# Seven half-size products for most pairs of the first layer's up tiles, and another order of attention's instructions, in a two-layer transformer kernel on one core

## The chip, the core and the metric

The kernel runs on one core of one Trainium2 chip. A core has five engines that each work through their own list of instructions in order: TensorE (PE, with its weight loads as PEld), VectorE (DVE), ScalarE (ACT), GpSimd (POOL) and SyncE (SP), which here only issues DMAs. They wait for each other by semaphores. The metric is the device time of one execution, in microseconds (us).

## The reference, cut to what matters

Two layers run over 768 tokens of 1024 features: 512 latent tokens and 256 context tokens. The second layer gives up the context tokens after its attention projections. The part that changes most is the channel sub-layer of the first layer:

```python
u = h @ w_up                                   # 768 x 1024 times 1024 x 5632
u = depthwise_conv3(u) + conv_b                # along the tokens
g, v = jnp.split(u, 2, axis=-1)                # 22 tiles of 128 gates, 22 of values
x = x + gate * ((jax.nn.silu(g) * v) @ w_down) # 2816 -> 1024
```

The mixing sub-layer before it (projections, grouped-query attention with 8 heads, differential attention with 4 heads, output projection) runs in both layers. Everything is float32. A layer's modulation (`adaLN`) is a product of a 1024-vector with 1024 x 6144 weights, of which most tiles are computed on VectorE beside other work.

## The kernel before

**Layout.** Features lie on the 128 partitions and tokens along the free dimension, so a tile of an activation is 128 x 768: tokens 0 to 511 (one PSUM bank) and 512 to 767 (another). There are eight banks of 512 floats, so four such pairs of banks.

**Float32 by three products.** TensorE takes each operand rounded (`fp32r`), so every operand is split in two: a high half made by ScalarE (`w_hi`, `h_hi`, `a_hi`: a copy that rounds) and a low half made by a subtraction (`w_lo` on GpSimd, line 1136; `h_lo` and `a_lo` on VectorE, lines 2255 and 2622). One product is then three matmuls, high by high, low by high and high by low: helper `three`, lines 1254 to 1256.

**The weight stream.** Units of 128 x 1024 floats (512 KB) come from HBM by SP (`load_unit`, line 1020) into two raw buffers `w_raw`. ScalarE makes `w_hi` (line 1700) and GpSimd `w_lo` in a ring of four. SP loads the next unit into a raw buffer when `w_lo` of the one in it is made. A unit is the weights of one 128-feature up tile, or of one down tile.

**The channel sub-layer.** `PARTS = [8, 8, 6]`: three times in a layer, `n` pairs of a gate tile and a value tile go up, and then eight down tiles sum over those `n` pairs. An up tile is `feature_unit`: for each of the two token groups, 8 k-tiles of three matmuls. For each pair (`pairs`, ScalarE from line 2061 and VectorE from line 2595):

- ScalarE: `conv_g` and `conv_v` from PSUM with the middle tap and the bias (line 2070), after `a_lo` of the pair before; then the next units' `w_hi`; the SiLU (line 2077) and `a_hi` (line 2079).
- VectorE: the outer taps, four instructions for a tile (line 2610); the product of gate and value (line 2619); `a_lo` (line 2622); and one tile of the modulation weights against two vectors (`ada_tile`, line 2117), whose 512 KB SP loads (line 1024) in its one queue with the weights.
- After the part's pairs, VectorE adds each down tile to `x_sb` (`update`, line 2560), with more tiles of the modulation beside it.

In the last part the last four down tiles (`tail_units`) are made for the first token group first, so that the norm of that group can begin while TensorE does the second.

**Attention.** `mixing_plan` writes down each operation of the mixing sub-layer with its engine, a duration, a preferred position and what it needs, and places them one by one: always the operation that can begin first, by those durations and a delay of .06 or .09 us for a signal. The order so found is what the four engines' lists contain. All waits are semaphores on what an operation needs, so the durations in the plan decide the order and nothing else.

## Time and profile before

| | us |
|---|---|
| median of 3 runs (1761.12 to 1761.82) | 1761.22 |
| the profiled execution | 1760.48 |
| its span in the profile | 1758.7 |
| PE busy | 1658.7 (94%) |
| DVE busy | 1120.0 (64%) |
| ACT busy | 769.9 (44%) |
| POOL busy | 617.5 (35%) |
| channel sub-layer of layer 0, stretch 480 to 1034 | 554 |
| attention of layer 0, stretch 105 to 405 | 300 |
| attention of layer 1, stretch 1063 to 1340 | 277 |

Busy is the time in which an engine had an instruction in work. Matmuls overlap each other in the profile, and their ends are modelled, so the pace of TensorE is read from the distance between the starts of two matmuls, not from the duration of one.

### The profile page before, as it was taken

How to read it: one execution, taken by the hardware profiler on the slowest of the kernel's cores; microseconds unless marked ns; L12 is line 12 of the kernel's file. 1: busy time of each engine (PE TensorE's matmuls, PEld its weight loads, DVE VectorE, ACT ScalarE, POOL GpSimd, SP SyncE). 2: the span in 40 equal slices, each digit the busy share in tenths (PEclk: the TensorE clock that was granted, in tenths of full speed). 3: DMA queues.
4: the chain of work that ended last, by engine and by line, in shares of the span. 5: the costliest groups of instructions: out<-in, count | busy, mean ns of one | idle time of the engine just before them, and what ended most of it. 6: DMA issues, size and time to landing. Idle time of an engine off the chain costs nothing.

```text
span 1758.7 us, 25943 instructions
## 1 busy us (share of the span) xinstructions
PE 1658.7 (94%) x9530; PEld 1403.9 (80%) x9530; DVE 1120.0 (64%) x1749; ACT 769.9 (44%) x1273; POOL 617.5 (35%) x311
## 2 busy tenths in 40 slices
PE   5999998889799999999999998999888999999997
PEld 3778786778688888888888886888666888888887
DVE  7986677677876575767245774677664864254256
ACT  6546676463253311332123344666554543243242
POOL 0356560210123243323422307564222154444442
PEclk9899999999899999999999999999999999999999
DMA  9520000024222333433434423000012133233232
GB/s 393 178 93 25 25 25 13 25 109 150 90 96 87 116 121 108 134 117 120 144 120 131 144 96 96 25 25 25 25 37 96 48 120 97 94 95 106 87 99 91
DMA packets 45533, 168.24 MB, mean 96 GB/s; under 512 B 4736, under 2 KB 6784, under 8 KB 43520
## 3 DMA queue, kind: packets, MB, share of 16 engines
q1 hardware_dynamic: 40896, 156.50, 26.4%
q10 hardware_dynamic: 4544, 10.49, 1.6%
q8 instruction: 60, 0.98, 0.2%
q14 instruction: 33, 0.27, 0.0%
HBM read 161.73 MB, written 5.24 MB: 95 GB/s over the span
## 4 chain that ended last, share of the span: by engine, by line
PE 73%; DVE 7%; issue 3%; ACT 2%; POOL 1%; DMA 1%; DVEq 0%; ACTq 0%; SPq 0%; POOLq 0%
PE ps L1254 22%; PE ps L1255 21%; PE ps L1256 21%; PE ps L1385 3%; PE ps L1399 2%; DVE junk_mid L2150 1%; PE ps L1418 1%; DVE sqsum L2220 1%; DVE nb L2408 1%; PE ps L1419 1%; DVE p_sb L2426 1%; POOL w_lo L1136 1%; ACT ptmp L1919 1%; DMA w_raw<-w_d 1%; DVE ht L2247 0%
## 5 line engine op out<-in xcount | busy, mean ns | idle before, releaser
L1136 POOL TENSOR_TENSOR w_lo<-w_raw,w_hi 128x1024 fp32r<-128x1024 f32 x175 | 444.3, 2541 | 933.2 <-ACT w_hi L1700 893.9
L1254 PE MATMUL ps<-h_hi,w_hi 128*128 128x512 f32 (+1 forms) x1592 | 570.3, 358 | 14.5 <-DVE h_lo L2255 6.8
L1255 PE MATMUL ps<-h_lo,w_hi 128*128 128x512 f32 (+1 forms) x1592 | 558.8, 351 | 0.0
L1256 PE MATMUL ps<-h_hi,w_lo 128*128 128x512 f32 (+1 forms) x1592 | 558.4, 351 | 0.0
L1254 PEld LDWEIGHTS ps<-h_hi,w_hi 128*128 128x128 f32 x1592 | 304.6, 191 | 63.4 <-issue 24.7
L1256 PEld LDWEIGHTS ps<-h_hi,w_lo 128*128 128x128 f32 x1592 | 304.2, 191 | 39.9
L1255 PEld LDWEIGHTS ps<-h_lo,w_hi 128*128 128x128 f32 x1592 | 305.1, 192 | 35.5
L1700 ACT ACTIVATE w_hi<-w_raw 128x1024 fp32r<-128x1024 f32 x188 | 198.3, 1056 | 240.8 <-PE ps L1256 222.5
L1254 PE MATMUL ps<-a_hi,w_hi 128*128 128x512 f32 (+1 forms) x552 | 191.8, 347 | 1.2 <-DVE a_lo L2622 1.2
L1255 PE MATMUL ps<-a_lo,w_hi 128*128 128x512 f32 (+1 forms) x552 | 191.5, 347 | 0.0
L1256 PE MATMUL ps<-a_hi,w_lo 128*128 128x512 f32 (+1 forms) x552 | 191.1, 346 | 0.0
L2610 DVE SCALAR_TENSOR_TENSOR conv_v<-ps,sm,conv_v 128x511 f32<-128x511 f32 (+1 forms) x132 | 83.2, 658 | 141.4 <-ACT conv_v L2070 135.1
L2408 DVE TENSOR_REDUCE nb<-ps 128x1 f32<-128x768 f32 (+1 forms) x160 | 129.1, 845 | 29.4 <-PE ps L1385 28.9
L1176 POOL TENSOR_TENSOR p_sb<-p_sb,ri 128x768 f32<-128x768 f32 (+1 forms) x80 | 107.5, 1363 | 93.5 <-DVE ri L2415 93.5
L2433 DVE TENSOR_TENSOR pt_lo<-ps,pt_hi 128x512 fp32r<-128x512 f32 (+1 forms) x160 | 106.3, 675 | 43.2 <-ACT pt_hi L1929 41.9
L2610 DVE SCALAR_TENSOR_TENSOR conv_g<-ps,sm,conv_g 128x511 f32<-128x511 f32 (+1 forms) x132 | 83.1, 658 | 68.9 <-ACT conv_g L2070 57.5
L1929 ACT ACTIVATE pt_hi<-ps 128x512 fp32r<-128x512 f32 (+1 forms) x160 | 91.9, 586 | 76.0 <-PE ps L1399 75.2
L2560 DVE SCALAR_TENSOR_TENSOR x_sb<-ps,mod,x_sb 128x512 f32<-128x512 f32 x72 | 45.3, 657 | 123.5 <-PE ps L1256 123.2
L2117 DVE CUSTOM_DVE_ANT_0 ada_junk<-ada_b,c_bc 128x1024 bf16<-128x1024 f32 x80 | 117.0, 1463 | 2.0 <-DMA ada_b<-ada_d 0.7
L1919 ACT ACTIVATE p_sb<-ps,nb 128x768 f32<-128x768 f32 (+1 forms) x120 | 97.0, 813 | 46.8 <-DVE nb L2408 43.3
L2070 ACT ACTIVATE conv_v<-ps,sm 128x512 f32<-128x512 f32 x66 | 44.2, 705 | 167.0 <-PE ps L1256 167.0
L1254 PEld LDWEIGHTS ps<-a_hi,w_hi 128*128 128x128 f32 x552 | 104.6, 190 | 14.7 <-DVE a_lo L2622 1.6
(186 smaller groups left out, 2414.1 us busy)
## 6 DMA issues: line engine op xcount, KB each, us to landing
w_raw<-w_d SPq DMA_DIRECT2D x188, 512.0 KB, 3.5
ada_b<-ada_d SPq DMA_DIRECT2D x56, 512.0 KB, 4.2
ada_first<-first_d SPq DMA_DIRECT2D x8, 1024.0 KB, 20.4
ada_lead<-ada_d SPq DMA_DIRECT2D x14, 512.0 KB, 3.6
ada_mid<-ada_d SPq DMA_DIRECT2D x10, 512.0 KB, 5.1
x_sb<-x_d SPq DMA_DIRECT2D x2, 1536.0 KB, 9.0
x_sb<-x_d ACTq DMA_DIRECT2D x1, 3072.0 KB, 11.9
x_spill_d<-x_sb ACTq DMA_DIRECT2D x1, 2048.0 KB, 7.8
```

Source lines behind the costliest of these rows:

```text
L1136: nc.gpsimd.tensor_tensor(w_lo[:, c % RING, :], w_raw[:, c % RAW, :], w_hi[:, c % RING, :].bitcast(f32), ALU.subtract).then_inc(w_lo_done, 1)
L1176: nc.gpsimd.tensor_tensor(buf, buf, ri[:, r:r + 1].broadcast_to([P, k]), ALU.mult).then_inc(scaled_done, 1)
L1254: nc.tensor.matmul(out, lh, rh, start=first, stop=False)
L1255: nc.tensor.matmul(out, lh, rl_, start=False, stop=False)
L1256: return nc.tensor.matmul(out, ll, rh, start=False, stop=last)
L1700: A(w_hi[:, c % RING, :], w_raw[:, c % RAW, :], ACT.Copy).then_inc(w_hi_done, 1)
L1919: A(dst, src, ACT.Exp, bias=nb[:, sid % 8:sid % 8 + 1], accum_out=total).then_inc(exp_done, 1)
L1929: A(pt_hi[tid % TURNS][:, 0:n], ps[:, 4 + tid % TURNS, 0:n], ACT.Copy).then_inc(pt_hi_done, 1)
L2117: ins = V.tensor_tensor_reduce(junk[:, :], buf[:, :], silu_c[:, s, :], 1.0, 0.0, ALU.mult, ALU.add, dst(s))
L2408: V.tensor_reduce(nb[:, sid % 8:sid % 8 + 1], src, AX.X, ALU.max, negate=True).then_inc(bias_done, 1)
L2433: V.tensor_tensor(lo[:, 0:n], ps[:, 4 + tid % TURNS, 0:n], hi[:, 0:n].bitcast(f32), ALU.subtract) \
L2610: ins = V.scalar_tensor_tensor(dst, src, sm[:, bass.ds(8 * i + w, 1)], dst, ALU.mult, ALU.add)
```

## The change

**Products.** `PARTS` becomes `[[4, 4, 4, 4, 3, 3], [8, 8, 6]]`. In layer 0 the first four pairs go as before. For the other 18 pairs the gate tile and the value tile are taken together as a 2 x 2 block product: tokens in two halves of 384, k in two halves of 4 k-tiles, and gate and value as the two columns. Instead of eight products of half size, seven are made, each 4 k-tiles x 3 matmuls of 384 columns:

```python
HALF = TOK // 2
PRODUCTS = ["a11 b11", "a22 t4", "s2 t2", "s1 t1", "a12 b21", "s3 t3", "s4 b22"]

def half_steps():
    steps = [("down", 0, d) for d in range(KT)]
    for part in range(1, len(PARTS[0])):
        a11, a22, s2, s1, a12, s3, s4 = PRODUCTS
        n = PARTS[0][part]
        for g in range(n):
            if g:
                steps += [(p, part, g) for p in (a11,)] + [(a22, part, g - 1)]
                steps += [(p, part, g) for p in (s2, s1, a12, s3, s4)]
            else:
                steps += [(p, part, g) for p in (a11, s1, s2, a12, s3, s4)]
        steps.append((a22, part, n - 1))
        steps += [("down", part, d) for d in range(KT)]
    return steps
```

**Sums of the activations**, once: `s1`, `s2`, `s4` (`sums_of_h`) in the four pairs of part 0, seven VectorE instructions of 384 columns for each of 4 k-tiles, then three roundings on ScalarE (`form_hi`) and three subtractions on VectorE (`sums_of_h_lo`); `s3` (`s3_of_h`, `s3_of_h_lo`) in the first four down tiles.

```diff
                             if l == 0:
-                                for j in range(per_pair):
-                                    a = ada0 + per_pair * half + j
-                                    at = half + 2 * j if part < 2 else 2 * half + j
-                                    ada_tile(a, 1 if part == 2 or j else 2, i, lambda s: ada_sum[:, s, at:at + 1],
-                                             2 * per_pair)
+                                ada_straight(5 * KT + half, 5 * KT + half + 1)
+                                if half:
+                                    sums_of_h_lo(half - 1)
+                                sums_of_h(half)
```

On ScalarE `form_hi` of the three sums stands behind the pair's high half (`glu_hi`), ahead of the next pair's `conv_g`.

**Sums of the weights**, for each of the 18 pairs: the pair's weights come as four quarters of 128 x 512 (256 KB), `b0` to `b3`, each with one raw place (`w_raw` cut in four). VectorE makes `t1` to `t4` of them. Every quarter or sum is one slot of a ring of eight, with its high half made by ScalarE (`half_hi`) and its low half by GpSimd, for `s1 t1` and `s4 b22` by VectorE. All of this is done seven steps ahead of the product.

```python
def t_sums(part, g):
    n = 4 * group_no(part, g)
    for role in range(3):
        dve.wait_ge(half_loaded[role], 16 * role_count(HALF_NO["b%d" % role, part, g]))
    ...
    t_sum_at(t_sum[1][:, :], half_raw(2), half_raw(1))
    dve.wait_ge(t_sums_done, n + 1)
    t_sum_at(half_raw(1), half_raw(1), half_raw(0))
    dve.wait_ge(t_sums_done, n + 2)
    t_sum_at(t_sum[0][:, :], half_raw(2), half_raw(1))

def made_ahead(s):
    ...
    kind, part, n = STEPS[s + AHEAD]
    if kind == "a11 b11":
        t_sums(part, n)
    elif kind in LO_DVE:
        half_lo(s + AHEAD)
    elif kind == "s3 t3":
        t_last(part, n)
```

SP may load a raw place again when its old content is used (`wait_role_read`): `b2` of the next pair when the low half for `s4 b22` is made, `b3` when the low half for `a22 t4` is made. Its queue, in the order of the steps:

```python
for s in range(-1, len(STEPS)):
    for r in range(max(s + AHEAD + 1, 0) if s >= 0 else 0, min(s + AHEAD + 2, len(STEPS))):
        for _ in loads_of(r):
            load_half(n)
            n += 1
    if s >= 0:
        for c in ADA_AT[s]:
            load_ada(c, 0)
```

**Putting the products together.** A product can add to what stands in PSUM. ScalarE copies one result to the place where the next is summed (`seed`, twice for a pair), and keeps `s1 t1` in SBUF (`keep`); VectorE adds it twice (`join`). ScalarE's list in the order of the steps:

```python
if kind == "a11 b11":
    if n: conv_start(part, n - 1, 1)
elif kind == "a22 t4":
    if n < PARTS[0][part] - 1: seed(part, n + 1, 0)
    else: conv_start(part, n, 1)
elif kind == "s2 t2":
    if n: conv_start(part, n - 1, 0)
    else: seed(part, n, 0)
elif kind == "s1 t1" and n:
    seed(part, n, 1)
elif kind == "a12 b21":
    if n == 0: seed(part, n, 1)
    keep(part, n)
    if n: gate_silu(part, n - 1)
half_hi(s + AHEAD)
if kind == "s3 t3" and n:
    gate_hi(part, n - 1)
```

VectorE's list in a pair's steps is: `join` of the pair before, `t_sums` of the next pair and the taps of the value; the taps of the gate (and in parts 3 to 5 a modulation tile); the low half for `s1 t1`; the product of gate and value; `t_last`; the low half of the result (`glu_lo`); `join`; the low half for `s4 b22`. TensorE waits in `product` for `seeded` ahead of `s2 t2` and `s3 t3`, for `joined` ahead of `a22 t4`, and for the taps.

**Down tiles** sum over 4 or 3 pairs, so there are 48 of them in layer 0 where there were 24, with as many matmuls in all and twice as many updates of `x_sb`. One modulation tile stands with each down tile of parts 1 to 3, one or two with those of part 4, and one with each of the first four of parts 0 and 5; those up to number 63 are for two vectors, the later for one.

**Attention.** The durations in `mixing_plan` are changed (a few of some 20), and so are the delays with which it places operations:

```diff
-        y["R1"] = op("POOL", "R1", 1.1, pos, [y["EV"][0], before, y["temps"]], y=y, before=before)
+        y["R1"] = op("POOL", "R1", 1.28, pos, [y["EV"][0], before, y["temps"]], y=y, before=before)
...
-                ex = op("ACT", "EX", 1.12 if wide else .58, at - .5, need, sid=sid, S=s, m=m, it=it, lane=lane,
+                ex = op("ACT", "EX", 1. if wide else .57, at - .5, need, sid=sid, S=s, m=m, it=it, lane=lane,
...
-            ready = [(max(now[e], max([n["end"] + n.get("lag", 0) + (.09 if n["eng"] != e else .06) for n in x["need"]],
-                                  default=0.)), x)
+            ready = [(max(now[e], max([n["end"] + SIGNAL[e] for n in x["need"]], default=0.)), x)
...
-        x["begin"], x["end"] = t, t + x["us"]
-        now[e] = x["end"]
+        x["begin"], x["end"] = t, t + x["us"] + DRAIN[e]
+        now[e] = t + x["us"] - OVERLAP[e]
```

**How the order moves, place 1: VectorE in a pair of part 0.** Before, from a pair's low half `a_lo` to the next loop turn's bookkeeping (`ada_junk` is the modulation tile, two vectors):

```order
L2619 TENSOR_TENSOR conv_g<-conv_g,conv_v 128x768
...
L2622 TENSOR_TENSOR a_lo<-conv_g,a_hi 128x768
...
L2117 ISA ada_junk,ada_sum<-ada_b_139,c_bc 128x1024
L2117 ISA ada_sum 128x1
...
L2117 ISA ada_junk,ada_sum<-ada_b_139,c_bc 128x1024
L2117 ISA ada_sum 128x1
```

And in the changed kernel, in the second pair (`form` are the sums of the activations, `s_hi` and `s_lo` their halves):

```order
L3285 TENSOR_TENSOR conv_g<-conv_g,conv_v 128x768
L3290 TENSOR_TENSOR glu_lo_134<-conv_g,glu_hi_130 128x768
L2589 ISA ada_junk,mod<-ada_b_161,c_bc 128x1024
...
L2704 TENSOR_TENSOR s_lo_126<-form_138,s_hi_123 128x384
L2704 TENSOR_TENSOR s_lo_127<-form_139,s_hi_124 128x384
L2704 TENSOR_TENSOR s_lo_128<-form_137,s_hi_125 128x384
L2695 TENSOR_TENSOR form_137<-h_hi,h_lo 128x384
...
L2700 TENSOR_TENSOR form_137<-form_137,form_139 128x384
L3276 SCALAR_TENSOR_TENSOR conv_g<-ps,sm,conv_g 128x511
```

Ten instructions of 384 columns now stand between a pair's modulation tile and the next pair's taps.

**Place 2: SP's queue and VectorE's list where part 2's down tiles end and part 3 begins.** SP before, in the down tiles of the first part, alternates between a weight unit and a modulation tile:

```order
L1020 DMA w_raw<-w_d 128x1024
L1024 DMA ada_b_139<-ada_d 128x1024
L1020 DMA w_raw<-w_d 128x1024
L1024 DMA ada_b_140<-ada_d 128x1024
L1020 DMA w_raw<-w_d 128x1024
```

SP now; the four quarters are `b0` to `b3` of part 3's second pair, and the modulation tile behind them is the one of the seventh down tile:

```order
L1238 DMA ada_b_161<-ada_d 128x1024 [waits ada_used]
L1229 DMA w_raw<-half_d 128x512 [waits half_lo_pool,t_sums_done]
L1229 DMA w_raw<-half_d 128x512 [waits half_lo_dve]
L1229 DMA w_raw<-half_d 128x512 [waits half_lo_dve,t_sums_done]
L1229 DMA w_raw<-half_d 128x512 [waits half_lo_pool]
L1238 DMA ada_b_160<-ada_d 128x1024 [waits ada_used]
L1238 DMA ada_b_161<-ada_d 128x1024 [waits ada_used]
```

VectorE at the same place, from the update of the seventh down tile (`w_lo` is the low half for `s4 b22` of the first pair, the last three rows are the sums for the second):

```order
L3230 SCALAR_TENSOR_TENSOR x_sb<-ps,mod,x_sb 128x512
L3230 SCALAR_TENSOR_TENSOR x_sb<-ps,mod,x_sb 128x256
L2661 TENSOR_TENSOR w_lo<-w_raw,w_hi 128x512
L2589 ISA ada_junk,mod<-ada_b_160,c_bc 128x1024
...
L2589 ISA ada_junk,mod<-ada_b_160,c_bc 128x1024
...
L3230 SCALAR_TENSOR_TENSOR x_sb<-ps,mod,x_sb 128x512
L3230 SCALAR_TENSOR_TENSOR x_sb<-ps,mod,x_sb 128x256
L2666 TENSOR_TENSOR t_sum_142<-w_raw 128x512
L2666 TENSOR_TENSOR w_raw<-w_raw 128x512
L2666 TENSOR_TENSOR t_sum_141<-w_raw 128x512
```

The load of the modulation tile stands behind the four quarters on SP, and the sums of the weights stand behind that tile on VectorE.

**Place 3: ScalarE at the beginning of layer 0's attention** (`p_sb` are exponentials, `pt_hi` high halves of turned probabilities, `b_raw` a projection's result, `w_hi` a weight unit). Before:

```order
L1919 ACTIVATE p_sb,rs<-ps,nb 128x768 x2
L1873 ACTIVATE kb_hi_82<-b_raw_108 128x768
L1846 ACTIVATE b_raw_109<-ps 128x512
L1919 ACTIVATE p_sb,rs<-ps,nb 128x768 x2
L1700 ACTIVATE w_hi<-w_raw 128x1024
L1846 ACTIVATE b_raw_109<-ps 128x256
```

And now:

```order
L2377 ACTIVATE p_sb,rs<-ps,nb 128x768
L2331 ACTIVATE kb_hi_82<-b_raw_108 128x768
L2377 ACTIVATE p_sb,rs<-ps,nb 128x768 x3
L2304 ACTIVATE b_raw_109<-ps 128x512
L2377 ACTIVATE p_sb,rs<-ps,nb 128x768 x2
L2387 ACTIVATE pt_hi_51<-ps 128x512
L2041 ACTIVATE w_hi<-w_raw 128x1024
```

The same operations stand in another order: here the first high half of turned probabilities comes ahead of the weight unit.

## Rows read from the trace of the kernel before

**Rows 1.** Busy time by stretch: channel sub-layer of layer 0, attention of both layers.

```profile
core 0: us, PE busy (x) PEld busy (x) DVE busy (x) ACT busy (x) POOL busy (x), PEclk, DMA share, GB/s
480.00:1034.00 554.00, 553.75 (x3194) 490.10 (x3193) 341.34 (x509) 175.62 (x236) 175.67 (x65) 1.00 0.36 121
...
105.00:405.00 300.00, 274.78 (x1854) 228.67 (x1853) 215.75 (x388) 183.08 (x380) 114.81 (x80) 0.97 0.11 36
1063.00:1340.00 277.00, 254.86 (x1609) 206.32 (x1608) 183.14 (x299) 158.99 (x297) 124.74 (x75) 0.97 0.12 37
```

**Rows 2.** Who waited for whom, 510 to 1030: us, times, longest.

```profile
ACT conv_v L2070 <- PE ps L1256: 117.8, 20, 6.1
...
DVE x_sb L2560 <- PE ps L1256: 54.4, 13, 6.1
```

**Rows 3.** Timeline of TensorE, one up tile: start us, us, engine, line.

```profile
556.46 0.40 PE L1254 MATMUL ps<-h_hi,w_hi 128*128 128x512 f32 x1
...
561.92 0.28 PE L1254 MATMUL ps<-h_hi,w_hi 128*128 128x256 f32 x1
```

**Rows 4.** Timeline of VectorE, the first pairs of layer 0's first part, and its fourth pair's low half.

```profile
507.61 1.14 DVE L2610 SCALAR_TENSOR_TENSOR conv_g<-ps,sm,conv_g 128x511 f32<-128x511 f32 x2 [8.09 <-ACT conv_g L2070]
508.91 1.14 DVE L2610 SCALAR_TENSOR_TENSOR conv_g<-ps,sm,conv_g 128x511 f32<-128x511 f32 x2 [0.16 <-DVE conv_g L2610]
...
518.49 2.42 DVE L2610 SCALAR_TENSOR_TENSOR conv_g<-ps,sm,conv_g 128x511 f32<-128x511 f32 x4
...
523.28 0.96 DVE L2619 TENSOR_TENSOR conv_g<-conv_g,conv_v 128x768 f32<-128x768 f32 x1
525.37 0.96 DVE L2622 TENSOR_TENSOR a_lo<-conv_g,a_hi 128x768 f32 x1 [1.14 <-ACT a_hi L2079]
526.25 1.22 DVE L2117 CUSTOM_DVE_ANT_0 ada_junk<-ada_b,c_bc 128x1024 bf16<-128x1024 f32 x1
...
555.06 0.96 DVE L2622 TENSOR_TENSOR a_lo<-conv_g,a_hi 128x768 f32 x1 [1.14 <-ACT a_hi L2079]
```

**Rows 5.** Timeline of ScalarE around the second pair of rows 4.

```profile
524.37 0.85 ACT L2079 ACTIVATE a_hi<-conv_g 128x768 f32 x1 [2.58 <-DVE conv_g L2619]
526.57 1.24 ACT L2070 ACTIVATE conv_g<-ps,sm 128x512 f32<-128x512 f32 x2 [1.36 <-DVE a_lo L2622]
```

**Rows 6.** Timeline of GpSimd and of VectorE around a pair's product.

```profile
700.87 2.41 POOL L1136 TENSOR_TENSOR w_lo<-w_raw,w_hi 128x1024 fp32r<-128x1024 f32 x1 [5.78 <-ACT w_hi L1700]
...
702.45 1.65 DVE L2619 TENSOR_TENSOR conv_g<-conv_g,conv_v 128x768 f32<-128x768 f32 x1
```

**Rows 7.** Groups by line and shape: busy us, mean ns of one, idle before.

```profile
L2449 DVE TENSOR_TENSOR oa_lo<-o_sb,oh 128x512 fp32r<-128x512 f32 x4 | 2.6, 685 | 0.0
L2433 DVE TENSOR_TENSOR pt_lo<-ps,pt_hi 128x256 fp32r<-128x256 f32 x8 | 3.4, 421 | 1.8 <-ACT pt_hi L1929 1.8
L1168 POOL TENSOR_TENSOR swapped<-swapped,tabs 128x512 f32<-128x512 f32 x26 | 33.6, 1293 | 3.1 <-DVE swapped L2360 3.0
L1929 ACT ACTIVATE pt_hi<-ps 128x512 fp32r<-128x512 f32 x152 | 89.0, 597 | 72.6 <-PE ps L1399 71.8 <-PE ps L1419 0.2
L2560 DVE SCALAR_TENSOR_TENSOR x_sb<-ps,mod,x_sb 128x512 f32<-128x512 f32 x48 | 35.9, 748 | 123.5 <-PE ps L1256 123.2 <-DVE mod L2633 0.2
L2560 DVE SCALAR_TENSOR_TENSOR x_sb<-ps,mod,x_sb 128x256 f32<-128x256 f32 x24 | 11.4, 475 | 0.0
```

**Rows 8.** DMA issues: KB each, median us from issue to landing.

```profile
w_raw<-w_d SPq DMA_DIRECT2D x188, 512.0 KB, 3.5
ada_b<-ada_d SPq DMA_DIRECT2D x56, 512.0 KB, 4.2
...
out_d<-y_sb ACTq DMA_DIRECT2D x8, 256.0 KB, 2.7
```

**Rows 9.** Busy time by stretch: layer 0's last down tiles, and a pause before its channel sub-layer.

```profile
1023.00:1046.00 23.00, 19.94 (x130) 17.10 (x129) 18.35 (x31) 11.85 (x19) 2.38 (x1) 1.00 0.39 138
460.00:480.00 20.00, 13.98 (x72) 13.10 (x70) 15.15 (x26) 5.70 (x10) 2.50 (x1) 0.65 0.13 38
```

More of the change, by code:

```diff
@@ new lines, with place_of, slot_of, slot_before @@
+STEPS = half_steps()
+STEP = {x: s for s, x in enumerate(STEPS)}
+LO_DVE = ("s1 t1", "s4 b22")
+def place_of(s):
+    return s + (-len(STEPS) % SLOTS if s >= STEP["down", len(PARTS[0]) - 1, 0] else 0)
+def slot_of(s):
+    return (SLOTS // 2 + place_of(s)) % SLOTS
+def slot_before(s):
+    p = place_of(s) - SLOTS
+    at = {place_of(r): r for r in range(s)}
+    while p >= 0 and p not in at:
+        p -= SLOTS
+    return at[p] if p >= 0 else (p + SLOTS) // 2 - RING
+def product_no(s):
+    return sum(x[0] != "down" for x in STEPS[:s + 1])
@@ L124, in unit_runs @@
+ADA_AT = ada_steps()
 def unit_runs(a, b):
@@ L2309, in tail @@
                 else:
-                    ahead = [c + RING + n for n in range(1, RING)]
+                    ahead = [UNITS[0] + RAW, UNITS[0] + RAW + 1]
                 if ahead:
```

710 lines of the change are left out of this document (598 added, 112 removed).

## The prediction, as it was put on record before the changed kernel was run

> **What bounds the kernel now.** I read first the busy time by stretch. In the channel sub-layer of layer 0 TensorE is busy in 553.75 of 554 us at full granted clock; VectorE works 341 us of it, ScalarE and GpSimd 176 each [rows 1]. The waits then say who waits for whom: ScalarE's `conv_v` 117.8 us and VectorE's update of `x_sb` 54.4 us, both for matmuls [rows 2]. So every matmul column taken away there is time, until VectorE, with 213 us free, or a chain through it becomes the bound. The two attentions are no such stretch: TensorE is idle 25.2 and 22.1 us in them [rows 1], which is all that another order could win.
>
> **Matmuls removed.** In an up tile 24 matmuls of 512 columns take 561.92 − 556.46 = 5.46 us, .2275 each [rows 3]; the same row-to-row distance with 24 of 256 gives .120, so a tile is 8.34 and a pair 16.68 us. A matmul of 384 should lie halfway, .174. A pair by seven products is 84 x .174 = 14.6 us; 18 pairs save 2.08 each, **−37.4**. The bounds: 384 at three quarters of the 512 (.1706) gives −42, at 1.5 times the 256 (.180) −28. The Trainium skill ("TensorE: Matmul & The Clock Gate", Back-to-back issue gap) has N / 2.4 + 2.5 ns instead: 162.5 ns, a pair in 13.65 us, and −54.5. But by it a 512 would take .216, and the rows show .2275, so they decide. Ten small matmuls that mark banks as written add 10 x .17: **+1.7**. The 48 down tiles hold as many matmuls as 24 did.
>
> **Part 0: VectorE becomes the bound.** Before, a pair takes it from the taps at 518.49 to the end of `a_lo` at 526.33, 7.85 us, and 2 x 1.22 for the modulation tile [rows 4]; the rest is slack. Now ten instructions of 384 columns follow (place 1). Between .421 for 256 and .685 for 512 [rows 7] one is .55, .48 with the next one's start overlapped, and dependent ones wait .16 [rows 4]: 5.3 us. ScalarE then rounds the sums before the next `conv_g`: .5, the eviction 1.24 [rows 5] and signals of .13 to .24 (the gaps between rows 4 and rows 5), 2.1. With half a microsecond of semaphore bookkeeping that is 18.2 us for a pair against TensorE's 16.7. VectorE starts its first taps at 507.6 [rows 4], late, since the first units finish together, and made this up before. Now it can't: the fourth `a_lo` ends at 507.6 + 3 x 18.2 + 7.85 = 570, where it ended at 556.0 [rows 4]. Behind it come a modulation tile and forms (7.7), and then four down tiles, each with a modulation tile of 2.4, an update of .75 + .475 less overlap [rows 7], and the fourth sum's three forms and low half 2.1: 5.6 each, against 4.2 of TensorE (12 x .3475). With the first weight sums (2.7) the fourth update ends at about 604. The eighth down tile can then end at 609, where TensorE alone would at 581 (the ups to 547.6, and 33.4): **+27**. I see nothing that hides it; its bounds are 20 (no bookkeeping, 17.5 for a pair) and 30.
>
> **Entries to parts 1 to 5.** Place 2 decides. A load of `b3` waits for the low half of the first pair's `a22 t4`, whose ring slot is free only when the last down tile D7 is multiplied; the seventh down tile's modulation stands behind that load on SP, and on VectorE ahead of the last update and of the next sums; ScalarE's high half of the next pair's `s2 t2` waits for those, and stands ahead of `seed`, for which the first pair's `s2 t2` waits. From D7's end, with signals of .2: high half .6 and low half on GpSimd 1.3 [rows 7], load 4.2 [rows 8], two vectors 2.4 [rows 4], update 1.15, three sums 2.1, high half .6, seed .5 and seven signals: 14.3 us. TensorE has only `a11` and `s1 t1` by then, 24 x .174 = 4.2. It stalls 10.1. In parts 4 and 5 the tile is for one vector, 9 each. In part 1 no modulation tile stands there, but the low halves and `b2`'s load after the late updates: about 8. Sum **+47**, bounds 42 and 55 (the load 3.5 and the low halves of the same engine in the way).
>
> **The groups' own loop.** Within a part VectorE has a closed round for each pair: low half for `s4 b22` made → SP loads `b2` of the next but one, 2.7 for 256 KB [rows 8] and two signals, 3.0 → three sums 2.1 → taps of value and gate 4.8 [rows 4] → ScalarE's SiLU .85 [rows 5] and two signals, 1.25 → product .96 → `t_last` .7 → `glu_lo` .96 → `join` .55 → low half .7. That is 15.0. Product and `glu_lo` also meet GpSimd's two low halves of 1.3. Such a meeting is in the trace: the product took 1.65 instead of .96, and ended with GpSimd's operation begun at 700.87 [rows 4, 6]. I take 2.2 for two meetings: **17.2 us against TensorE's 14.6** (bounds 15.0 and 17.6), and in parts 3 to 5 1.2 more for a modulation tile. The 13 rounds inside parts give 6 x 2.6 + 7 x 3.8 = 42; five entries each hand over some 2 us of start (−10); the last low half of the three-pair parts comes 2.3 after TensorE has run out of other k-tiles (+4.6): **+37**. The Trainium skill ("SBUF — State Buffer", SBUF: two separate sides) calls the meeting an exclusive lock of one port pair, held for a whole instruction. Rows 6 agree; what it would do at its worst is a rival below.
>
> **End of the layer, clock, attention.** Four final down tiles of three pairs give the norm of the first token group less matmul cover: half of 8.6, of which 2 show: **+2** (3 us are idle there now [rows 9]). A pause of some 6 us in 20 goes with a granted clock of .65 [rows 9]: matmuls after it run at 1.2 instead of 2.4 GHz. The new stalls of 10 us make about five such places, 2 us each: **+10** (0 to 20). Attention's reorder moves no work; I give it **−8** of the 47 idle us, bounds 0 and −20.
>
> **Sum**: −37.4 + 1.7 + 27 + 47 + 37 + 2 + 10 − 8 = +79.3. From the profiled execution's 1760.5, .04% under the median, that is 1840 us.
>
> **Rivals.**
> 1. *Faster.* The weight sums and the modulation loads keep ahead, so TensorE stays the bound: 1760.5 − 37.4 + 1.7 − 8 = 1717. The place is SP's queue at each D7. It decides from the point where all stalls together stay under 43.7 us, that is, if the entries fell from 9 to 3 us each and VectorE's rounds to 15. For it: VectorE's busy time would still be under 500 of 520 us. Against it: `b3` can't be loaded before D7 by any timing, and the entries alone come to 47. Chance .08.
> 2. *Entries and part 0 alone.* `b2` lands early or GpSimd's halves fall beside VectorE's waits, so rounds stay near 15: only some 6 of the 37 remain, and with a clock term of 5, 1804 us or, with 10 fewer at the entries, 1794. For it: the bounds of the round begin at 15.0. Chance .20.
> 3. *The lock at its worst.* If each of the two low halves always excludes VectorE's two-operand work and also delays the sums (three 1.3 us meetings more a round), the round is 21 us: 13 x 3.9 = +51, 1891 us. The page named above would allow it. Against it: in rows 4 to 6 only one product in sight is stretched. Chance .12.
> 4. *It does nothing in sum*: within 3.5 us, for which stalls of 44 are needed, .02.
>
> The forecast as worked has the other .58. About .2% (3.5 us) is what a measurement here can tell from no change. Faster by more .08, within .02, slower .90. The range takes in rival 2 and the bounds of the sum (20 + 42 + 15 on one side, 30 + 55 + 50 on the other): 1788 to 1890.
>
> **What would show it.** In the changed kernel's first channel stage: starts of 384-column matmuls .174 apart; TensorE's `s2 t2` of each part's first pair waiting 8 to 10 us for ScalarE's `seed`, five times; VectorE waiting some 6 us for `ada_b` ahead of each part's last update; pairs 17 to 19 us apart, not 14.6; the first part's down tiles ending near 609; a granted clock under 1.00 there. Wrong would be: TensorE busy over 97% of the stage (rival 1), or pairs 14.6 to 15.2 apart with stalls only at entries (rival 2), or attention's stretches shorter by over 10 us each.

## The result, and the profile after

The changed kernel takes 1863.99 us (median of 4 runs, 1858.52 to 1867.39) against 1761.17 (1760.23 to 1761.82) before: ratio 1.0582, 95% interval 1.0569 to 1.0594. It is 103 us slower; the forecast was 1840, range 1788 to 1890. The four runs lie 8.9 us apart, so a difference of a few us from their median, further down, is uncertain by some 2 us each way. The profiled execution is the fastest of the four, 1858.5 us with a span of 1856.4.

Busy time by stretch of the changed kernel: its channel stage in layer 0, and the entry to part 3. The last three columns are the granted clock, the DMA share and GB/s.

```profile
core 0: us, PE busy (x) PEld busy (x) DVE busy (x) ACT busy (x) POOL busy (x), PEclk, DMA share, GB/s
483.00:1139.00 656.00, 551.45 (x2991) 508.99 (x2991) 491.22 (x736) 236.07 (x383) 213.24 (x144) 0.94 0.31 102
835.00:853.00 18.00, 9.13 (x32) 8.65 (x33) 11.38 (x18) 2.40 (x6) 1.72 (x2) 0.54 0.46 139
```

The stage took 554 us, with TensorE never idle [rows 1]; it now takes 656, TensorE is idle for 105 of them, and VectorE has gone from 341 us to 491. What TensorE waited for there, in us, times, longest:

```profile
PE ps L1497 <- ACT ps L2213: 44.2, 15, 9.5
PE ps L1497 <- DVE x_sb L3230: 25.0, 9, 4.1
PE ps L1497 <- DVE ps L2756: 10.3, 7, 3.1
PE ps L1497 <- DVE conv_g L3276: 8.4, 1, 8.4
PE ps L1454 <- DVE sqsum L2890: 4.7, 1, 4.7
```

L2213 is ScalarE's `seed`, L3230 VectorE's update of `x_sb`, L2756 its `join`, L3276 the taps of part 0. In rows 2 the arrows pointed the other way: ScalarE and VectorE waited for TensorE. VectorE itself isn't busy all the time. What it waited for longest in the stage are the loads of modulation tiles (26.1 us; .7 in the whole kernel before), and in `t_last` GpSimd's low halves:

```profile
DVE ada_junk L2589 <- DMA ada_b<-ada_d: 26.1, 6, 7.9
DVE w_raw L2666 <- POOL w_lo L1372: 24.8, 9, 4.7
```

TensorE at part 3's entry, and then in a group of part 2, start and duration:

```profile
835.34 0.66 PE L1497 MATMUL ps<-s_hi,w_hi 128*128 128x384 f32 x1 [3.95 <-DVE x_sb L3230]
...
848.37 0.69 PE L1497 MATMUL ps<-s_hi,w_hi 128*128 128x384 f32 x1 [8.53 <-ACT ps L2213]
848.86 0.53 PE L1498 MATMUL ps<-s_lo,w_hi 128*128 128x384 f32 x1
849.18 0.53 PE L1499 MATMUL ps<-s_hi,w_lo 128*128 128x384 f32 x1
```

```profile
745.25 0.33 PE L1497 MATMUL ps<-h_hi,w_hi 128*128 128x384 f32 x1
745.43 0.33 PE L1498 MATMUL ps<-h_lo,w_hi 128*128 128x384 f32 x1
745.60 0.33 PE L1499 MATMUL ps<-h_hi,w_lo 128*128 128x384 f32 x1
```

Where nothing waits, a matmul of 384 starts every .173 us. Behind a wait the starts are .32 apart: the granted clock of that stretch averages .54, which is 1.2 GHz for most of it.

To account for the whole I took the distance between the starts of each two matmuls in the stage and compared it with .2275, .120 and .1738 us for 512, 256 and 384 columns: what is beyond by more than .45 us is a wait, and the small rest is counted as low clock. Against the profiled execution of before (the stage took 553.7 and has 655.6 now, +101.9):

| term | predicted | measured |
|---|---|---|
| fewer columns, with the marking matmuls | −35.7 | −34.7 |
| part 0, first taps to the last down tile | +27 | +21.6 |
| entries to parts 1 to 5 | +47 | +52.3 (7.2, 13.2, 13.0, 7.4, 11.4) |
| rounds inside the parts | +37 | +25.2 |
| end of the layer | +2 | +11.8 |
| low clock behind the waits | +10 | +25.9 |
| attention's order (stage begins 3.1 later, all behind it 7.3 shorter) | −8 | −4.2 |
| sum | +79.3 | +97.9 |

The remaining 5 us to the median are between this execution and the others, and no profile of those was taken.

### The profile page after: what moved, and what is told of

Its sections match the earlier page's. It is cut to its first block, busy times and chain, and to the rows that moved or that the text cites. A ratio compares the mean times of both kernels' runs of the same rounds, so it can differ in the third digit from the quotient of the medians.

```text
span 1856.4 us, 25601 instructions
## 1 busy us (share of the span) xinstructions
PE 1655.3 (89%) x9329; PEld 1421.0 (77%) x9329; DVE 1272.3 (69%) x1975; ACT 829.1 (45%) x1419; POOL 651.9 (35%) x390
## 4 chain that ended last, share of the span: by engine, by line
PE 36%; DVE 8%; issue 3%; ACT 2%; POOL 2%; DMA 1%; DVEq 0%; SPq 0%; ACTq 0%; POOLq 0%
PE ps L1497 11%; PE ps L1498 10%; PE ps L1499 10%; PE ps L1628 2%; PE ps L1642 2%; POOL w_lo L1356 1%; PE ps L1661 1%; DMA ada_b<-ada_d 1%; DVE ada_junk L2589 1%; DVE conv_v L2767 1%; DVE sqsum L2890 1%; PE ps L1662 1%; DVE t_sum L2666 1%; DVE conv_g L2767 0%; DVE ht L2917 0%
## 5 line engine op out<-in xcount | busy, mean ns | idle before, releaser
L1497 PE MATMUL ps<-h_hi,w_hi 128*128 128x512 f32 (+2 forms) x1304 | 476.8, 366 | 28.5 <-DVE ps L2756 10.3
L1356 POOL TENSOR_TENSOR w_lo<-w_raw,w_hi 128x1024 fp32r<-128x1024 f32 x116 | 281.8, 2433 | 624.7 <-ACT w_hi L2041 585.0
L1498 PE MATMUL ps<-h_lo,w_hi 128*128 128x512 f32 (+2 forms) x1304 | 463.1, 355 | 0.0
L1499 PE MATMUL ps<-h_hi,w_lo 128*128 128x512 f32 (+2 forms) x1304 | 462.6, 355 | 0.0
L1372 POOL TENSOR_TENSOR w_lo<-w_raw,w_hi 128x512 fp32r<-128x512 f32 (+1 forms) x102 | 144.1, 1424 | 263.7 <-ACT w_hi L2059 263.6
L1497 PE MATMUL ps<-glu_hi,w_hi 128*128 128x512 f32 (+1 forms) x352 | 121.7, 346 | 30.7 <-DVE x_sb L3230 15.4
L2059 ACT ACTIVATE w_hi<-w_raw 128x512 fp32r<-128x512 f32 (+1 forms) x138 | 83.9, 612 | 117.4 <-PE ps L1499 57.1
L2589 DVE CUSTOM_DVE_ANT_0 ada_junk<-ada_b,c_bc 128x1024 bf16<-128x1024 f32 x80 | 116.1, 1452 | 27.1 <-DMA ada_b<-ada_d 26.1
L3230 DVE SCALAR_TENSOR_TENSOR x_sb<-ps,mod,x_sb 128x512 f32<-128x512 f32 x120 | 72.4, 636 | 80.1 <-PE ps L1499 80.1
L1497 PE MATMUL ps<-s_hi,w_hi 128*128 128x384 f32 x216 | 79.1, 366 | 52.6 <-ACT ps L2213 43.1
L1498 PE MATMUL ps<-glu_lo,w_hi 128*128 128x512 f32 (+1 forms) x352 | 120.5, 342 | 0.0
L1499 PE MATMUL ps<-glu_hi,w_lo 128*128 128x512 f32 (+1 forms) x352 | 120.0, 341 | 0.0
```

The costliest lines, as they stand in the source:

```text
L1356: nc.gpsimd.tensor_tensor(w_lo[:, c % RING, :], w_raw[:, c % RAW, :], w_hi[:, c % RING, :].bitcast(f32), ALU.subtract).then_inc(w_lo_done, 1)
L1372: nc.gpsimd.tensor_tensor(half_slot(w_lo, s)[:, 0:width], half_source(s), half_slot(w_hi, s)[:, 0:width].bitcast(f32), ALU.subtract).then_ ...
L1497: nc.tensor.matmul(out, lh, rh, start=first, stop=False, skip_group_check=onto)
L1498: nc.tensor.matmul(out, lh, rl_, start=False, stop=False, skip_group_check=onto)
L1499: return nc.tensor.matmul(out, ll, rh, start=False, stop=last, skip_group_check=onto)
L2589: ins = V.tensor_tensor_reduce(junk[:, :], buf[:, :], silu_c[:, s, :], 1.0, 0.0, ALU.mult, ALU.add, dst(s))
```

## Experiments

### Attention's order alone, and the products with the old order

The first run is the kernel before with the whole new plan, of which these lines are a part; the second is the changed kernel with the old plan.

```diff
-        y["R1"] = op("POOL", "R1", 1.1, pos, ...
+        y["R1"] = op("POOL", "R1", 1.28, pos, ...
...
-        x["begin"], x["end"] = t, t + x["us"]
-        now[e] = x["end"]
+        x["begin"], x["end"] = t, t + x["us"] + DRAIN[e]
+        now[e] = t + x["us"] - OVERLAP[e]
```

> The kernel before with the new durations and delays in attention's plan, nothing else. The prediction gave the reorder -8 us, which is 1753. The changed kernel's trace has layer 0's channel stage beginning 3.1 us later than before and all behind it 7.3 us shorter, which would make -4, 1757, if the two parts of the change don't touch each other. The rival: attention's order is worth nothing by itself (within 2 us, 1761) and both differences belong to what stands next to it.

> The changed kernel with the old durations in attention's plan. If the two parts add up, it stands as far above the changed kernel as the plan alone stands below the kernel before: +4, 1868. The rival is that it is within 2 us of the changed kernel, 1864, or faster than it.

Measured: 1758.06 us (11 runs) against 1761.41, ratio .9984, interval .9975 to .9993; and 1867.64 us (5 runs) without it in the changed kernel, 3.65 above the changed kernel's median. The new order alone is worth 3.4 us (1.2 to 4.4 by the interval). The second run agrees with two parts that add, but its 3.65 us is small beside the 8.9 us between the changed kernel's runs. The order loses time in layer 0 and wins twice as much in layer 1. TensorE's first matmul of the channel stage, before and with the plan alone:

```profile
480.36 0.47 PE L1254 MATMUL ps<-h_hi,w_hi 128*128 128x512 f32 x1 [0.15 <-DVE h_lo L2255]
```

```profile
484.11 0.47 PE L1257 MATMUL ps<-h_hi,w_hi 128*128 128x512 f32 x1 [0.67 <-DVE h_lo L2258]
```

From the end of the stage on the plan alone is 7.3 us shorter, the same as in the changed kernel. The plan alone is also the fastest kernel of this study, if by two tenths of a per cent.

### The modulation load ahead of the quarters

```diff
+            early = {STEP["down", part, KT - 2] for part in range(1, len(PARTS[0]) - 1)}
             for s in range(-1, len(STEPS)):
+                if s in early:
+                    for c in ADA_AT[s] + ADA_AT[s + 1]:
+                        load_ada(c, 0)
...
-                if s >= 0:
+                if s >= 0 and s not in early and s - 1 not in early:
```

> SP loads the modulation tiles of the seventh and eighth down tile of parts 1 to 4 ahead of the next part's b0 to b3. Theory (the load behind b3 holds the last update, the sums, the high half and the seed): in part 3's entry VectorE could go on at 835.8 at once and the seed ends near 842.5 where it ended at 848.3, so 5.5 us at each of four entries and some of the slow clock behind them, 25 us in all: 1839. Rival (VectorE's own work and GpSimd's low halves are what is late, the load only stands beside them): under 5 us, 1860.

Measured: 1843.98 us (ratio 1.047, 1.0454 to 1.0486), 20 below the changed kernel. The chain of the prediction is real: VectorE's waits for modulation tiles, 26.1 us in the changed kernel, are 1.0 in this one. It can be read in the changed kernel at part 3's entry, where the last down tile ends at 829.0. VectorE: update of the seventh down tile, low half, modulation tile, last update, last of three sums:

```profile
834.06 1.13 DVE L3230 SCALAR_TENSOR_TENSOR x_sb<-ps,mod,x_sb 128x512 f32<-128x512 f32 x2
835.12 0.69 DVE L2661 TENSOR_TENSOR w_lo<-w_raw,w_hi 128x512 fp32r<-128x512 f32 x1
841.61 1.23 DVE L2589 CUSTOM_DVE_ANT_0 ada_junk<-ada_b,c_bc 128x1024 bf16<-128x1024 f32 x1 [5.81 <-DMA ada_b<-ada_d]
...
844.03 1.14 DVE L3230 SCALAR_TENSOR_TENSOR x_sb<-ps,mod,x_sb 128x512 f32<-128x512 f32 x2
...
846.53 0.69 DVE L2666 TENSOR_TENSOR t_sum<-w_raw 128x512 f32<-128x512 f32 x1
```

And ScalarE, the high half for `s2 t2` and the seed:

```profile
847.31 0.63 ACT L2059 ACTIVATE w_hi<-t_sum 128x512 fp32r<-128x512 f32 x1 [15.80 <-DVE t_sum L2666]
847.85 0.47 ACT L2213 ACTIVATE ps<-ps 128x384 f32<-128x384 f32 x1
```

The seed begins 18.9 us behind the last down tile, and TensorE goes on 19.4 us behind it (848.37). SP's queue at the same place, the last two quarters and the modulation tile:

```profile
835.88 0.81 SPq L1229 DMA_DIRECT2D w_raw<-half_d  x2
836.72 0.43 SPq L1238 DMA_DIRECT2D ada_b<-ada_d  x1
```

Here the prediction had `b3` waiting for GpSimd's low half of `a22 t4`. That ended at 835.26. SP stood until 835.88, one place earlier in its queue, at `b2`, which needs VectorE's low half for `s4 b22` (835.12 to 835.81, above). VectorE held its own load, though GpSimd, done .55 us earlier, would have held it nearly as long. With the load ahead the 5.8 us for `ada_b` are gone, but TensorE's wait for the seed in part 3 falls only from 8.5 to 5.2 and the one for the update from 4.0 to 3.0.

### The seeds ahead of the high halves

```diff
-                        else:
-                            seed(part, n, 0)
-                    elif kind == "s1 t1" and n:
-                        seed(part, n, 1)
+                    elif kind == "s1 t1":
+                        seed(part, n, int(n > 0))
```

> ScalarE copies the seed of each part's first pair ahead of the high half of the next pair's s2 t2, not behind it; nothing else moves. Theory (TensorE's s2 t2 waits only for the seed, which waits only for its place in ScalarE's list): the waits of 3.8, 8.9, 8.5, 7.3 and 9.5 us for the seed go, 38 us, and 5 to 10 us of low clock behind them: 1818. The wait of 4 us for an update ahead of s1 t1 stays. Rival (the late high half then stops TensorE some products later, at the second pair's s2 t2): half of it comes back, 1840.

Measured: 1845.2 us (1.0481, 1.0464 to 1.0497): 19 down, not 46. The rival's size, though not its place: the wait moves one product on, to the second seed, which stood behind the same high half. TensorE in part 3 (the kernel with the first seed moved), and ScalarE just before it:

```profile
846.09 0.66 PE L1497 MATMUL ps<-h_hi,w_hi 128*128 128x384 f32 x1 [5.11 <-ACT ps L2213]
```

```profile
844.42 0.63 ACT L2059 ACTIVATE w_hi<-t_sum 128x512 fp32r<-128x512 f32 x1 [17.01 <-DVE t_sum L2664]
844.96 0.61 ACT L2059 ACTIVATE w_hi<-w_raw 128x512 fp32r<-128x512 f32 x1
845.48 0.47 ACT L2213 ACTIVATE ps<-ps 128x384 f32<-128x384 f32 x1
```

So the second seed went ahead as well:

```diff
                     elif kind == "a12 b21":
                         if n == 0:
                             seed(part, n, 1)
                         keep(part, n)
                         if n:
                             gate_silu(part, n - 1)
+                        else:
+                            half_hi(s + AHEAD - 2)
+                            half_hi(s + AHEAD - 1)
-                    half_hi(s + AHEAD)
+                    if n or kind not in ("s1 t1", "s2 t2"):
+                        half_hi(s + AHEAD)
```

> ScalarE makes both seeds and the kept copy of a part's first pair ahead of the high halves for the second pair's s2 t2, s1 t1 and a12 b21. With the first seed alone moved, 5.4, 5.3, 3.7 and 4.6 us of wait for ScalarE showed at the next product that needs the second seed. Theory (the same queue, one place on): these 19 us go and some 4 us of low clock: 1822. Rival (the high halves come so late that TensorE stops at the second pair instead): within 5 us of the run with the first seed moved, 1842.

Measured: 1845.28 us (1.0473, 1.0454 to 1.0492), no gain at all over one seed. The waits for seeds are down to 5.8 us in the whole stage, and TensorE's longest waits are now for VectorE's `join`, ahead of the first pair's `a22 t4`:

```profile
PE ps L1497 <- DVE ps L2758: 34.3, 13, 6.4
PE ps L1497 <- DVE x_sb L3232: 23.6, 9, 5.0
```

The theory that the seed's place in ScalarE's list is all that costs at the entries falls with this pair of runs: the first seed's place was worth 19 us, and what the second's would have given came back at a third place, where TensorE waits for VectorE. Why VectorE is late the pair doesn't say. It has much work there, but in both kernels it still stands idle for the modulation loads, 26.9 us with one seed moved and 28.5 with both. Part 3's entry with both:

```profile
841.09 1.23 DVE L2591 CUSTOM_DVE_ANT_0 ada_junk<-ada_b,c_bc 128x1024 bf16<-128x1024 f32 x1 [6.44 <-DMA ada_b<-ada_d]
```

The next runs take this idle time away.

### VectorE's order at the entries

With both seeds ahead, the seventh down tile's modulation is loaded ahead of the quarters, and VectorE does the modulation of the last three down tiles behind the last update and the sums:

```diff
                         made_ahead(s)
-                        for c in ADA_AT[s]:
-                            ada_straight(c, c + 1, streams=2 if c < N_ADA + 2 * KT else 1)
+                        late = 0 < part < len(PARTS[0]) - 1
+                        for r in (range(s - 2, s + 1) if late and n == KT - 1 else () if late and n >= KT - 3 else (s,)):
+                            for c in ADA_AT[r]:
+                                ada_straight(c, c + 1, streams=2 if c < N_ADA + 2 * KT else 1)
```

> Both seeds first as in the run beside it; the seventh down tile's modulation is loaded ahead of b0 to b3, and on VectorE the modulation of down tiles six to eight of parts 1 to 4 stands behind the eighth update and the three sums. Theory (VectorE comes to each entry with modulation work that nobody waits for): the waits of 3 to 5 us ahead of s1 t1 for the seventh update go too, 13 us and 5 us of low clock more than with both seeds alone: 1804. Rival (three modulation tiles in a row then delay VectorE's low halves and the first join): 1818 or more.

Measured: 1829.57 us (1.0392, 1.0374 to 1.0409), 34 below the changed kernel and 16 below both seeds alone; 1804 was expected, and this is the rival's side of it (1818 or more). VectorE's waits for the loads are down to 3.7 us. TensorE's waits of 4 us for the update are down to .6, but those of 5 to 6 us for the join stayed. VectorE at part 3's entry in this kernel, from the last sum to the join, and TensorE:

```profile
829.30 1.22 DVE L2595 CUSTOM_DVE_ANT_0 ada_junk<-ada_b,c_bc 128x1024 bf16<-128x1024 f32 x1
...
830.55 2.20 DVE L2595 CUSTOM_DVE_ANT_0 ada_junk<-ada_b,c_bc 128x1024 bf16<-128x1024 f32 x1
...
838.64 1.22 DVE L2595 CUSTOM_DVE_ANT_0 ada_junk<-ada_b,c_bc 128x1024 bf16<-128x1024 f32 x1
...
842.27 0.56 DVE L2762 TENSOR_TENSOR ps<-ps,shared 128x384 f32<-128x384 f32 x1
```

```profile
842.97 0.66 PE L1501 MATMUL ps<-h_hi,w_hi 128*128 128x384 f32 x1 [6.39 <-DVE ps L2762]
```

VectorE isn't idle for more than .3 us between 826.3 and 843, though three of its six modulation instructions from 829.3 to 839.8 took 2.1 to 2.2 us instead of 1.22, all beside GpSimd's low halves. So here the amount of work ahead of the join, stretched or not, is what TensorE waits for; the next run puts that to the test by taking work away.

```diff
+                    k = 16 if s and short else D
-                    ins = V.tensor_tensor_reduce(junk[:, :], buf[:, :], silu_c[:, s, :], ...
+                    ins = V.tensor_tensor_reduce(junk[:, 0:k], buf[:, 0:k], silu_c[:, s, 0:k], ...
```

> The run with the reordered entries, with the modulation tiles of the down tiles of parts 1 and 2 for one vector and 16 of the 1024 features of the other, so 16 times some 1.1 us less on VectorE; this leaves out part of the modulation. Theory (after the reorder VectorE's amount of work ahead of the first join is what TensorE waits for, 5.3 and 6.6 us in parts 2 and 3): those two waits go with the low clock behind them, 14 us: 1815. Rival (a chain through GpSimd's low halves and the loads): within 4 us of 1829.6.

Measured: 1815.76 us (1.0309, 1.0292 to 1.0327), 13.8 below the reordered entries: the 14 of the theory. Both waits for the join are gone (part 2 has no wait above 1.6 us left), and the granted clock of the stage is .98 where the reordered entries had .96 and the changed kernel .94:

```profile
485.00:1096.00 611.00, 540.77 (x2990) 496.27 (x2991) 478.01 (x734) 233.75 (x382) 209.30 (x144) 0.98 0.34 109
```

16 instructions of 1.1 us each less on VectorE, 17.6 us, gave 13.8 us. At these two entries, once the load is out of the way, VectorE's work is TensorE's time, to some four fifths.

### Part 0

```diff
+                            if l == 0 and half:
+                                for f in range(3):
+                                    form_hi(3 * (half - 1) + f, form[(1, 2, 0)[f]][:, :], s_hi[f][:, half - 1, :])
                             act.wait_ge(bank_read, 4 * i + (evac_index(up_unit(l, part) + 2 * half) + 1))
                             A(conv_g[:, 0:T], conv_g[:, 0:T], ACT.Silu).then_inc(silu_done, 1)
...
-                            if l == 0:
+                            if l == 0 and half == 3:
                                 for f in range(3):
```

> In part 0 ScalarE rounds the sums of the activations behind the next pair's conv_g and conv_v, not ahead of them. Theory of the prediction (2.1 us a pair between VectorE's last form and its next taps, and VectorE bounds part 0): the wait of 1.7 us for conv_g, shown twice at full length, goes, the pair's round falls from 17.8 to 16 us, and the down tiles begin 5 us earlier: 1858. Rival (TensorE's down tiles wait for VectorE's updates and forms, however early the pairs end): within 2 us, 1863.

Measured: 1864.4 us (1.0591, 1.0574 to 1.0609), nothing. From one `glu_lo` to the next it was 16.3, 17.7 and 16.8 us in the changed kernel and is 17.9, 15.5 and 18.3 here: the middle round won what was expected, and the others gave it back. For the last the trace says how. VectorE and GpSimd in this kernel:

```profile
555.80 4.70 DVE L2707 TENSOR_TENSOR s_lo<-form,s_hi 128x384 fp32r<-128x384 f32 x3
```

```profile
555.40 4.69 POOL L1372 TENSOR_TENSOR w_lo<-w_raw,w_hi 128x512 fp32r<-128x512 f32 x3 [4.65 <-ACT w_hi L2059]
```

The same three subtractions took 1.49 us in the changed kernel. Here they and GpSimd's three low halves (1.3 each alone) lay in the same 5 us, and VectorE lost 3.2. This reads one trace; no run took GpSimd's work away to show it. Since the pairs as a whole got no shorter, the run doesn't decide between its theory and its rival.

The same shortening of the modulation as above, in the changed kernel's part 0 (first line: pairs; second: its first four down tiles):

```diff
-                                ada_straight(5 * KT + half, 5 * KT + half + 1)
+                                ada_straight(5 * KT + half, 5 * KT + half + 1, short=True)
...
-                            ada_straight(c, c + 1, streams=2 if c < N_ADA + 2 * KT else 1)
+                            ada_straight(c, c + 1, streams=2 if c < N_ADA + 2 * KT else 1, short=not part)
```

> The changed kernel with part 0's eight modulation tiles for one vector and 16 features of the other, which leaves out part of the modulation. Theory (VectorE's throughput bounds part 0 from its first taps to the fourth update): 8 x 1.1 us less on VectorE come back whole, 1855. Rival (waits on ScalarE and GpSimd bound it, as the later rounding of the sums suggested by bringing nothing): under 3 us, 1861.

Measured: 1855.12 us (1.0534, 1.0516 to 1.0552), 8.9 below the changed kernel, as the theory has it (8 x 1.1). From the first matmul of the stage to that of part 1 it took 128.1 us in the changed kernel and takes 119.8. Part 0 is bound by VectorE's throughput.

### The end of the layer

```diff
-                            if n >= RAW:
-                                unit_hi(UNITS[0] + n - RAW)
                             act.wait_ge(bank_read, evac_index(c) + 1)
                             square_x(n, 2, 0, TOK, squares_base(2) + n)
+                            if n >= RAW:
+                                unit_hi(UNITS[0] + n - RAW)
```

> In the last part's first down tiles ScalarE squares x_sb ahead of the high half of the next layer's unit, whose load waits behind four modulation tiles on SP. Theory (the unit's load holds the square, the square VectorE's sum, that the fourth update, and that TensorE's bank): the 3.8 us wait of VectorE for the square and as much of TensorE's 4.3 go, 5 us in all: 1859. Rival (the missing cover of three-pair down tiles is the cause, whatever the order): within 2 us, 1863.

Measured: 1858.15 us (1.0551, 1.0531 to 1.0571), 5.8 below, with both kernels' runs far apart (1855.7 to 1861.2 here). In the changed kernel the sum of squares waited for ScalarE, which stood at the high half of a unit that SP came to only at 1110.5, behind four modulation tiles. VectorE and SP of the changed kernel:

```profile
1116.83 2.48 DVE L2890 TENSOR_TENSOR sqsum<-sqsum,sqt 128x768 f32<-128x768 f32 x1 [3.76 <-ACT sqt L2282]
```

```profile
1086.90 23.46 SPq L1238 DMA_DIRECT2D ada_b<-ada_d  x4
1110.46 0.85 SPq L1234 DMA_DIRECT2D w_raw<-w_d  x2
```

With the edit the wait for the square is .5 us. TensorE no longer stands 4.1 us for the fourth update, but 8.5 us for the sum of squares instead of 4.7, since it comes there earlier and VectorE's modulation and biases are still ahead. From the first of these down tiles to the sum of squares it took 26.5 us (1103.70 to 1130.17) and takes 24.3: the two profiles show 2.2 us of the 5.8 in this place, and don't say where the others lie.

### Two attempts at a better version

The first has the reordered entries, the square first, and the modulation tiles of the last two down tiles spread into the first pair (a part of its edit is shown); the second also moves the last part's four tiles into parts 1 and 2.

```diff
                     elif kind == "a12 b21":
...
+                        if n == 0 and part > 1:
+                            for c in ADA_AT[STEP["down", part - 1, KT - 2]]:
+                                ada_straight(c, c + 1, streams=2 if c < N_ADA + 2 * KT else 1)
```

The second run's own edit:

```diff
-        tiles = [int(n < KT - PARTS[0][0]), 1, 1, 1, 1 + (n < 2), int(n < 4)][part]
+        tiles = [int(n < KT - PARTS[0][0]), 1, 1, 1, 1 + (n < 2), 0][part]
-            tiles = int(part >= 3)
+            tiles = int(part >= 3 or n >= 2)
```

> Reordered entries and ScalarE's square ahead of the next layer's unit, and VectorE takes the seventh and eighth down tile's modulation only where the first pair's a12 b21 and s4 b22 are, the latter behind the first join. Theory (the join is late because three modulation tiles stand ahead of it): the waits of 5.3, 6.6 and 2.8 us for it shrink by two thirds, 10 us, and the square's 6 us add: 1813. Rival (VectorE is short of time there in any order, and the tiles delay the next sums): only the square's 6, 1823.

> As the run beside it, and the four modulation tiles of the last part's down tiles are done in the third and fourth pair of parts 1 and 2, which moves every later tile four places on and leaves part 2's last four with one vector. Theory (the rounds of 14.1 us have room and the last down tiles don't): 5 us at the end of the layer and 4 in part 3's entry, less 2 in the groups: 7 us under the run beside it, 1806. Rival: the rounds get longer than 14.6 and it is even.

Measured: 1824.62 us (1.0353, 1.0336 to 1.0371) and 1824.9 us (1.0357, 1.034 to 1.0374). Both times the rival: the first is 5.0 us below the reordered entries, about the square's share and no more, the second gains nothing. In the first TensorE's wait for the join in part 3 went from 6.4 to 2.3 us, and one of 4.5 for a seed came behind it; in the second the waits inside parts 1 and 2 grew by 2.2 each (3.7 us where it was 1.5) and ate what part 3's entry and the last down tiles won. Moving modulation about inside this stage doesn't make VectorE's sum smaller.

## Why the prediction was right, and where its terms were off

The sum, +79.3, was 19 us short of the +97.9 read from the two profiles. The last down tiles (9.8), the clock (15.9), the entries (5.3), attention (3.8) and the columns (1.0) were priced too low by 35.8 in all, part 0 (5.4) and the rounds (11.8) too high by 17.2. That the total is off by no more than 19 us is in part luck, since the two sides cancel.

**The direction and the mechanism** hold: less TensorE time than was bought with VectorE time. The bound moved from the one engine to the other, as the first part of the prediction said it would when VectorE's free 213 us run out. It didn't need the whole 213: VectorE is busy in 491 of 656 us, and what counts is where its work and its waits lie, at the entries and in part 0.

**Columns.** 384 columns at .174 was read off two other shapes and measured .173; the saving, −34.7 with 15 marking matmuls where I counted 10, is 1 us off. An estimate by the Trainium skill's formula ("TensorE: Matmul & The Clock Gate", Back-to-back issue gap) is .1625, and no stretch of this trace shows that.

**Part 0.** Predicted from 18.2 us a round; the rounds measured 16.3, 17.7 and 16.8, and the last down tile ended at 608.4, where 609 was given, though the stage had begun 3 us later. The term is 5 us too large. The run with part 0's modulation shortened confirms its cause, VectorE's throughput. Taking away the 2.1 us between forms and taps that I put into it gave nothing: what one round won the others lost.

**Entries.** +47 against +52.3 (my own five figures add to 46, not 47), with the chain step by step as written. At part 3 it is 19.4 us long instead of 14.3. The load itself landed 4.9 us after its issue, near the 4.2 taken; most of the rest is that SP came to it at 836.7, 7.7 us after the last down tile instead of 3, held by VectorE's own low half. The stall that I gave as one of 10.1 us is two, 4.0 for the seventh update, which I hadn't listed, and 8.5 for the seed; in part 1 the seed's is only 3.8. The chain as the one cause holds for its first half: with the load cut out 20 us came back of the 25 expected. With the first seed cut out it was 19 of 46, and with the second nothing more. What "it stalls 10.1" as a sum along one path left out is a second path just behind the first: with the load ahead TensorE still waits 3.0 and 5.2 us at part 3's entry, and in the reordered kernel this is VectorE's amount of work.

**Rounds.** +37 against +25.2. The length of a round with weight sums in it was right, how many there are was wrong. VectorE's products of gate and value in part 2, and one in part 3:

```profile
756.75 0.96 DVE L2778 TENSOR_TENSOR conv_g<-conv_g,conv_v 128x768 f32<-128x768 f32 x1 [0.31 <-ACT conv_g L2196]
...
774.36 0.96 DVE L2778 TENSOR_TENSOR conv_g<-conv_g,conv_v 128x768 f32<-128x768 f32 x1 [0.32 <-ACT conv_g L2196]
...
788.50 0.96 DVE L2778 TENSOR_TENSOR conv_g<-conv_g,conv_v 128x768 f32<-128x768 f32 x1 [2.06 <-ACT conv_g L2196]
```

```profile
871.02 2.04 DVE L2778 TENSOR_TENSOR conv_g<-conv_g,conv_v 128x768 f32<-128x768 f32 x1
```

17.6 us, as the 17.2 of the sum, then 14.1: the second round has no weight sums in it, since the part has no pair left to make them for (the next part's come in the down tiles). The 13 rounds inside parts should have been 3, one in each four-pair part: 17.6 us twice and 18.5 in part 3, against 14.6, make 9.9 us. That the term was off by 12 us and not by 27 is luck. What filled most of the gap are waits that I had not listed, .7 to 3.2 us for a seed, a join or a low half in nearly every pair. The longest, for a join in part 5 (1090.0), comes behind a VectorE that stood idle itself, 2.8 us for ScalarE's `glu_hi`. Inside the round I had the wrong instructions stretched. In part 2 product and `glu_lo` kept their .96, and the sums took the time, `t_last` 1.76 instead of .69 after 1.19 us of waiting for GpSimd:

```profile
776.50 1.76 DVE L2666 TENSOR_TENSOR w_raw<-w_raw,t_sum 128x512 f32<-128x512 f32 x1 [1.19 <-POOL w_lo L1372]
```

No run took anything out of the rounds, so what these waits come from is read off the trace and not shown. The 2.7 us for the load of a quarter were read off a store [rows 8]; the loads measured 2.7 as well.

**End of the layer.** +2 against +11.8: the largest miss in proportion. I costed the missing cover of TensorE and not the queue: ScalarE's high half of the next layer's unit stands ahead of a square, and its load behind four modulation tiles on SP. A reading of SP's queue as at place 2 would have found it. The run with the square first gave 5.8 back, of which the traces show 2.2 here; by its trace the rest is VectorE's modulation and biases ahead of the tail, which no run tried.

**Clock.** +10 (0 to 20) against +25.9. I priced one pause for each entry at 2 us. The entries have up to two long waits each, and 1.9 to 3.4 us of slow matmuls, 13.9 in all; the last down tiles have 4.9, part 0's first down tile 1.7, and a join in part 3 and one in part 5 1.5 each. With waits taken away the clock comes back (.98 in the stage), so it is a consequence of them.

**Attention.** −8 against −4.2 in the profiles and −3.4 and −3.7 in the two comparisons.

**Rivals.** The "faster" one needed stalls under 43.7 us; they were 111 us above before's, without the clock. Of rival 3, the lock that also delays the sums: the sums of part 2, the product in part 3 and modulation instructions (2.16 and 2.20 us for 1.22) show it at full length, each beside one of GpSimd's low halves. But a round with it is 17.6 us, not the 21 of the rival. The Trainium skill ("SBUF — State Buffer", SBUF: two separate sides) has this as an exclusive lock held for a whole instruction, and these rows and the 4.70 us of the run on part 0 agree. It isn't new here, though: the modulation instruction's mean is 1452 ns now and was 1463 before, where VectorE had time to spare. No run separates what the lock costs.

## What to carry to other kernels

An algebraic saving on the engine that bounds is worth its size only if the engines that pay for it have time at the moments where they pay; count their work by stage, not over the span. When a wait sits at the end of a chain, ask for the second-longest path before pricing its removal: here moving both seeds gave 19 us where the first alone had been priced at 46. An engine that is late may be short of time or may itself be waiting; look at its idle time first. Here VectorE was both, and once its wait for a load was gone, 17.6 us of work less gave 13.8. And the long pauses that a change opens are followed by slow matmuls, which cost a quarter of the waits again here (25.9 us to 111).

## What the runs showed of the hardware

- A matmul of 384 float32 columns starts .173 us after the one before at the full clock and .32 us at the lower one. Halfway between the .120 and .2275 us of 256 and 512 columns [rows 3] is .174.
- Slow matmuls followed 13 of the stage's 38 waits of TensorE over .45 us; those waits were 2.1 to 9.7 us long. Behind the other 25, of .7 to 3.3 us, the granted clock stayed at 1.00. In part 0's down tiles, for one, behind 3.3 us at 596.9 and 2.9 at 604.1 it was 1.00, and behind 8.5 us at 564.6 it was .50.
- VectorE and GpSimd can stretch each other by more than the one meeting of [rows 6] had shown: three subtractions of 384 columns took 4.70 us beside three of GpSimd's and 1.49 without.
- A load of 256 KB landed in 2.7 us (median of 104) and one of 512 KB in 3.2 (median of 128). The load that VectorE waited 5.8 us for took 4.9 of them; issued earlier in SP's queue, the same loads cost VectorE 1.0 us in the whole kernel instead of 26.1, while its waits for quarters grew from 8.0 to 13.6.
